# Attention heads of a hybrid encoder: a new order on VectorE and ScalarE, and second copies read from SBUF

## What is computed

```python
proj = h @ w_in                                # h is (528, 1024), w_in (1024, 3072)
q, k, v = split(proj, 3)                       # 8 heads; q, k: 2 components of 64; v: 128
for s0 in range(0, L, Q_BLOCK):
    mask = cid[None, :ke] <= cid[s0:e0, None]  # chunks of 64 tokens, block-causal
    sc = einsum('bqhcd,bkhcd->bhcqk', q[:, s0:e0], k[:, :ke])
    p = softmax(where(mask, sc, -inf), axis=-1)
    attn = p[:, :, 0] - lam * p[:, :, 1]
    outs.append(einsum('bhqk,bkhe->bqhe', attn, v[:, :ke]))
o = o * rsqrt(mean(o * o, axis=-1) + SUBLN_EPS)
o = o * head_gain * (1.0 - lambda_init)
return o @ w_out
```

## Time and profile before

| | |
|---|---|
| median of 3 runs | 1328.1 us (1328.01 to 1328.35) |
| the profiled execution, own time | 1331.93 us |
| its span | 1330.3 us |
| mean granted TensorE clock | 0.991 |
| TensorE busy | 1262.3 us, 95% |
| VectorE busy | 701.1 us, 53% |
| ScalarE busy | 562.1 us, 42% |
| GpSimd busy | 77.5 us, 6% |

### The profile page before, as it was taken

How to read it: one execution, slowest core, us unless ns; L and a number is a source line. 1 busy time by engine, 2 the same in 40 slices (tenths; PEclk the granted TensorE clock), 3 DMA queues, 4 the chain that set the end, 5 groups by cost and what they waited for, 6 DMA issues and landing times.

```text
span 1330.3 us, 20889 instructions
## 1 busy us (share of the span) xinstructions
PE 1262.3 (95%) x8341; PEld 1151.7 (87%) x8341; DVE 701.1 (53%) x1034; ACT 562.1 (42%) x927; POOL 77.5 (6%) x104
## 2 busy tenths in 40 slices
PE   7899999999999999999988888888999999999997
PEld 6899999999999999999977777776788888888886
DVE  5867777654334334345556666664744343343443
ACT  4556656534123123133355666664542232231333
POOL 3311221110000000000100000000000000000000
PEclk9899999999999999999999999999999999999999
DMA  6342251222323222222321111121323223232221
GB/s 163 91 102 75 64 117 65 84 80 96 96 69 100 87 95 95 95 67 91 95 64 49 48 47 47 47 63 49 95 93 97 86 99 101 86 103 95 81 77 64
DMA packets 141574, 110.28 MB, mean 83 GB/s; under 512 B 22104, under 2 KB 139920, under 8 KB 141520
## 3 DMA queue, kind: packets, MB, share of 16 engines
q1 hardware_dynamic: 140000, 104.93, 25.7%
q0 software_dynamic: 1392, 4.49, 1.5%
q10 hardware_dynamic: 128, 0.09, 0.0%
HBM read 107.38 MB, written 2.13 MB: 82 GB/s over the span
## 4 chain that ended last, share of the span: by engine, by line
PE 74%; issue 20%; DVE 3%; ACT 1%; POOL 0%; DMA 0%; DVEq 0%; POOLq 0%; ACTq 0%
PE ps L1282 70%; PE ps L1331 3%; PE ps L1348 1%; DVE wl L864 0%; DMA meta_in<-in_meta_tokens_dram 0%; DVE yl L906 0%; PE ps L1380 0%; PE ps L1412 0%; DVE plo L973 0%; PE ps L1401 0%; PE ps L1434 0%; PE ps L1298 0%; DVE h L891 0%; DVE dmat L962 0%; DVE fin L1264 0%
## 5 line engine op out<-in xcount | busy, mean ns | idle before, releaser
L1282 PE MATMUL ps<-yh,wh 128*128 128x264 f32 (+1 forms) x1472 | 368.9, 314 | 1.4 <-DVE wl L864 0.8
L1282 PE MATMUL ps<-yl,wh 128*128 128x264 f32 (+1 forms) x1472 | 362.6, 310 | 0.0
L1282 PE MATMUL ps<-yh,wl 128*128 128x264 f32 (+1 forms) x1472 | 361.7, 310 | 0.0
L504 ACT ACTIVATE wh<-raw 128x1024 fp32r<-128x1024 f32 x192 | 200.2, 1050 | 189.1 <-PE ps L1282 188.7
L864 DVE TENSOR_TENSOR wl<-raw,wh 128x1024 fp32r<-128x1024 f32 x192 | 240.4, 1256 | 58.2 <-ACT wh L504 56.1
L1282 PE MATMUL ps<-ah,wh 128*128 128x264 f32 (+1 forms) x960 | 258.0, 323 | 1.5 <-DVE al L1253 0.8
L1282 PE MATMUL ps<-al,wh 128*128 128x264 f32 (+1 forms) x960 | 257.4, 322 | 0.0
L1282 PE MATMUL ps<-ah,wl 128*128 128x264 f32 (+1 forms) x960 | 256.5, 321 | 0.0
L1282 PEld LDWEIGHTS ps<-yh,wh 128*128 128x128 f32 x1472 | 240.9, 190 | 17.9 <-issue 2.1
L1282 PEld LDWEIGHTS ps<-yl,wh 128*128 128x128 f32 x1472 | 240.6, 190 | 13.1 <-issue 0.2
L1282 PEld LDWEIGHTS ps<-yh,wl 128*128 128x128 f32 x1472 | 240.1, 190 | 13.6
(11 more groups left out here) (213 smaller groups left out, 1086.8 us busy)
## 6 DMA issues: line engine op xcount, KB each, us to landing
raw<-in_mlp_w_up_dram SPq DMA_DIRECT2D x32, 1024.0 KB, 5.3
raw<-in_mlp_w_down_dram SPq DMA_DIRECT2D x32, 1024.0 KB, 4.9
raw<-in_diff_w_in_dram SPq DMA_DIRECT2D x24, 512.0 KB, 3.7
raw<-in_mlstm_w_in_dram SPq DMA_DIRECT2D x16, 512.0 KB, 3.9
raw<-in_mlstm_w_in_dram SPq DMA_DIRECT2D x16, 256.0 KB, 4.2
raw<-in_mlstm_w_out_dram SPq DMA_DIRECT2D x3, 1024.0 KB, 4.8
raw<-in_diff_w_out_dram SPq DMA_DIRECT2D x3, 1024.0 KB, 4.9
mbc<-gate_rows POOLq DMA_DIRECT2D x8, 264.0 KB, 4.4
```

Of the source, the lines that this page charges most:

```text
L504: return nc.scalar.activation(o, i, ACT.Copy, scale=scale)
L1282: last = mm(ps[:, bank + s, 0:w_], w[:, slot, kb, :], m[:, kb, t0:t0 + w_], start=(kb == 0 and n == 0), stop=(kb == CB - 1 and n == 2))
```

## The change

The diff of the kernel. In words: ScalarE's second copies of `vmeta` and `att_meta` read the first copy in SBUF and wait for it, with semaphores of their own (`vm_dup`, `meta_dup`) that TensorE waits for, while `vt_rd1` and `meta_rd` are now raised by the first copies. On ScalarE `qm` and the next q's weight split move behind the exponentials of block 2, and `turned` of block 2 ahead of the second `keys_hi`. On VectorE the maxima of block 0 and the low half of block 3 move to the end of the step before; meta's low half goes before the v weights' split; q's evacuation goes between the maxima and the weights of block 1; the maxima of block 2 go before `qlo`; the split of the next q's weights goes behind the maxima of block 3. On TensorE one more block of q is done ahead of the scores of block 1, and the last one directly behind them, before `output`.

```diff
--- before.py
+++ after.py
@@ -287,8 +287,8 @@
         max_done = [sem(f"max_done{c}") for c in range(2)]
         exp_done = [sem(f"exp_done{c}") for c in range(2)]
         rden_rd, e1_rd, attn_rd, at_t, at_rd, atl_rd = sems("rden_rd e1_rd attn_rd at_t at_rd atl_rd")
-        mask_base, mask_half, mask_made, qm_done, vtl_rd1, metal_rd = sems(
-            "mask_base mask_half mask_made qm_done vtl_rd1 metal_rd")
+        mask_base, mask_half, mask_made, qm_done, vtl_rd1, metal_rd, vm_rd1, vm_dup, meta_dup = sems(
+            "mask_base mask_half mask_made qm_done vtl_rd1 metal_rd vm_rd1 vm_dup meta_dup")
         lam_dve, lam_act = sems("lam_dve lam_act")
 
         hg_done, fsum, fln, frs, fmul_act, fmul_dve = sems("hg_done fsum fln frs fmul_act fmul_dve")
@@ -767,9 +767,10 @@
                 if exists(hd):
 
                     act.wait_ge(v_t1, hd + 1)
-                    copy(vth1[par][:, :, :], ps[:, B_TR1, :].rearrange("p (s e) -> p s e", e=P))
-                    copy(vmeta[par][0:16, :], ps[0:16, B_TR1 + 1, 0:P])
-                    copy(vmeta[par][32:48, :], ps[0:16, B_TR1 + 1, 0:P]).then_inc(vt_rd1, 1)
+                    copy(vth1[par][:, :, :], ps[:, B_TR1, :].rearrange("p (s e) -> p s e", e=P)).then_inc(vt_rd1, 1)
+                    copy(vmeta[par][0:16, :], ps[0:16, B_TR1 + 1, 0:P]).then_inc(vm_rd1, 1)
+                    act.wait_ge(vm_rd1, hd + 1)
+                    copy(vmeta[par][32:48, :], vmeta[par][0:16, :].bitcast(F32)).then_inc(vm_dup, 1)
                     if exists(n1):
                         split_unit(n1 * 3 + (U_IN1 + 2), 2, 1, n1)
                     else:
@@ -779,8 +780,9 @@
                 if exists(hd - 1):
 
                     act.wait_ge(meta_t, hd)
-                    copy(att_meta[0:16, :], ps[0:NMETA, B_TR1, :])
-                    copy(att_meta[64:80, :], ps[0:NMETA, B_TR1, :]).then_inc(meta_rd, 1)
+                    copy(att_meta[0:16, :], ps[0:NMETA, B_TR1, :]).then_inc(meta_rd, 1)
+                    act.wait_ge(meta_rd, hd)
+                    copy(att_meta[64:80, :], att_meta[0:16, :].bitcast(F32)).then_inc(meta_dup, 1)
                 if exists(hd):
                     for c in range(2):
                         scores(hd * 4 + 1, 1, c)
@@ -803,6 +805,11 @@
                         b0 = 64 * c
                         last = copy(qst[1 - par][c][b0:b0 + 64, :], qf1[b0:b0 + 64, NMETA:T], SCORE_SCALE)
                     last.then_inc(qhi_done, 1)
+                if exists(hd):
+                    for c in range(2):
+                        scores(hd * 4 + 2, 2, c)
+                    turned(hd, hd * 4 + 1, 1)
+                if exists(n1):
                     for c in range(2):
                         b0 = 64 * c
                         last = copy(qm[1 - par][c][b0:b0 + 64, :], qf1[b0:b0 + 64, NMETA:T], SCORE_SCALE)
@@ -810,10 +817,6 @@
                     split_unit(n1 * 3 + (U_IN1 + 3), 0, 1, n1 + 1)
                 elif exists(hd):
                     split(U_OUT1 + 3, 3, 1)
-                if exists(hd):
-                    for c in range(2):
-                        scores(hd * 4 + 2, 2, c)
-                    turned(hd, hd * 4 + 1, 1)
                 if exists(n1):
 
                     act.wait_ge(evac, n1 * 3 + (U_IN1 + 2))
@@ -821,10 +824,9 @@
                 if exists(hd):
                     for c in range(2):
                         scores(hd * 4 + 3, 3, c)
+                    turned(hd, hd * 4 + 2, 2)
                 if exists(n1):
                     keys_hi(par, 1)
-                if exists(hd):
-                    turned(hd, hd * 4 + 2, 2)
                 if exists(hd - 1):
 
                     act.wait_ge(ssq_done1, hd)
@@ -1177,6 +1179,7 @@
                 dve.wait_ge(vt_rd1, hd + 1)
                 V.tensor_tensor(vtl1[par][:, :, :], ps[:, B_TR1, :].rearrange("p (s e) -> p s e", e=P),
                                 vth1[par][:, :, :].bitcast(F32), ALU.subtract)
+                dve.wait_ge(vm_rd1, hd + 1)
                 V.tensor_tensor(vmeta[par][64:80, :], ps[0:16, B_TR1 + 1, 0:P],
                                 vmeta[par][0:16, :].bitcast(F32), ALU.subtract).then_inc(vtl_rd1, 1)
 
@@ -1189,39 +1192,32 @@
             def step1(hd, par, pair):
                 n1 = hd + 1
                 if exists(hd):
-                    maxima(hd * 4, 0)
-                if exists(hd - 1):
-                    turned_lo(hd * 4 - 1, 3)
-                if exists(hd):
                     values_lo(hd, par)
                     weights(hd, hd * 4, 0)
+                if exists(hd - 1):
+                    meta_lo(hd - 1)
                 if exists(n1) and exists(hd):
                     split(n1 * 3 + (U_IN1 + 2), 2)
                 elif exists(hd):
                     split(U_OUT1 + 2, 2)
-                if exists(hd - 1):
-                    meta_lo(hd - 1)
                 if exists(hd):
                     maxima(hd * 4 + 1, 1)
-                    weights(hd, hd * 4 + 1, 1)
                 if exists(n1):
 
                     scaled(n1 * 3 + U_IN1, 0, SEQ, qf1[:, :],
                            ps[:, 4 if isinstance(hd, int) and hd < 0 else B_Q1, :])
                 if exists(hd):
+                    weights(hd, hd * 4 + 1, 1)
                     turned_lo(hd * 4, 0)
+                    maxima(hd * 4 + 2, 2)
                 if exists(n1):
-                    split(n1 * 3 + (U_IN1 + 3), 0)
                     dve.wait_ge(qhi_done, n1 + 1)
                     for c in range(2):
                         b0, b1 = 64 * c, 64 - 64 * c
                         last = V.scalar_tensor_tensor(qst[1 - par][c][b1:b1 + 64, :], qf1[b0:b0 + 64, NMETA:T], SCORE_SCALE,
                                                       qst[1 - par][c][b0:b0 + 64, :].bitcast(F32), ALU.mult, ALU.subtract)
                     last.then_inc(qlo_done, 1)
-                elif exists(hd):
-                    split(U_OUT1 + 3, 3)
-                if exists(hd):
-                    maxima(hd * 4 + 2, 2)
+                if exists(hd):
                     weights(hd, hd * 4 + 2, 2)
                     turned_lo(hd * 4 + 1, 1)
                 if exists(n1):
@@ -1231,6 +1227,9 @@
                     maxima(hd * 4 + 3, 3)
                 if exists(n1):
                     keys_lo(n1, par, 0)
+                    split(n1 * 3 + (U_IN1 + 3), 0)
+                elif exists(hd):
+                    split(U_OUT1 + 3, 3)
                 if exists(hd):
                     weights(hd, hd * 4 + 3, 3)
                 if exists(n1):
@@ -1246,6 +1245,10 @@
                     wait(dve, v_t1, n1)
                     scaled(n1 * 3 + (U_IN1 + 2), 0, ALL, vf1[:, :],
                            ps[:, 2:4, 0:HALF] if isinstance(hd, int) and hd < 0 else None)
+                    maxima(n1 * 4, 0)
+                if exists(hd):
+                    turned_lo(hd * 4 + 3, 3)
+                if exists(n1):
                     split(n1 * 3 + (U_IN1 + 4), 1)
                 if exists(hd - 1):
 
@@ -1509,6 +1512,8 @@
             def output(n, par):
 
                 pe.wait_ge(metal_rd, n + 1)
+                pe.wait_ge(meta_dup, n + 1)
+                pe.wait_ge(vm_dup, n + 1)
                 mm(ps[:, B_PV1, :], vmeta[par][:, :], att_meta[:, :], start=True, stop=False)
                 for s in range(4):
                     for m, (v, w) in enumerate(((vth1, ath), (vth1, atl), (vtl1, ath))):
@@ -1583,18 +1588,19 @@
                         out_part(3, 0, 3)
                 if exists(hd):
                     if nxt:
-                        part(n1, 0, 5, 6)
+                        part(n1, 0, 5, 7)
                     scores(hd * 4 + 1, 1, par)
-                if exists(hd - 1):
-                    output(hd - 1, 1 - par)
-                if exists(hd):
                     if nxt:
-                        part(n1, 0, 6, CB)
+                        part(n1, 0, 7, CB)
                     elif last_head:
                         out_part(0, 5, 6)
                         out_part(1, 0, 1)
+                if exists(hd - 1):
+                    output(hd - 1, 1 - par)
+                if exists(hd):
 
                     wait(pe, metal_rd, hd)
+                    wait(pe, meta_dup, hd)
                     wait(pe, vtl_rd1, hd + 1)
                     turn(hd * 4, 0)
                 if nxt:
```

More of the change, by code:

```diff
@@ L1585, in step1 @@
                     if nxt:
-                        part(n1, 0, 5, 6)
+                        part(n1, 0, 5, 7)
                     scores(hd * 4 + 1, 1, par)
+                    if nxt:
+                        part(n1, 0, 7, CB)
+                    elif last_head:
+                        out_part(0, 5, 6)
+                        out_part(1, 0, 1)
                 if exists(hd - 1):
@@ L1590, in step1 @@
                 if exists(hd):
-                    if nxt:
-                        part(n1, 0, 6, CB)
-                    elif last_head:
-                        out_part(0, 5, 6)
```

(2 more changed lines are left out.)

## The result

The changed kernel takes 1280.67 us in the median (1280.51 to 1282.83, 4 runs), the kernel before 1328.22 us: a ratio of 0.9641, 95% interval 0.9623 to 0.9658. The direction held, and the stalls went as forecast, though the one before the product not by the filler that was given for it. One term, the pure work of a head, was 1 us too large, and it counts seven times.

A forecast was written before the change was run, and what follows sets the result against it. TensorE was taken as the only engine near its limit, losing time to stalls in the attention heads. Gains of 0.75 + 6.3 + 4.0 + 24.1 + 4.7 = 39.9 us took 1328.1 to 1288.2 us, range 1282 to 1306.

The forecast's parts named there:

- the pure work of a head: Steady head on TensorE: length of 31.27 us less 5.2 us standing still, taken as 26.05 us.
- Maxima of block 0 and low half of block 3: Value turning starts 2.6 us after the head's first scores (L), against 4.05; its stall shrinks from 1.62 to 0.1-0.2 us.
- Copies: ScalarE's second value and meta copies, reading SBUF: 0 to 0.3 us more ScalarE time per head, 0.2 taken, beside other work.
- Filler: Six more matmuls before block 1's scores, three after: product 3.1 us after the meta turning (M), its 1.18 us stall gone.
- Block 1's turn: TensorE turning block 1's weights: a new stall of 0.5 us a head, bounds 0 and 1.0.
- Block 2: Earlier maxima and exponentials remove stalls of 1.46 us before block 3's scores and 0.77 before turning block 2's weights.
- The ends: Gains outside heads 2 to 6: 0.75 us before head 0, 6.3 in it, 4.0 in head 1, 4.7 in the last.
- 1 (the clock falls all the same): Clock still falls in head 0 or the last head, costing 2.7 or some 1.7 us: 1291 to 1293 us, chance 12%.
- 2 (stalls half return): Slipping queues bring back 2 to 2.5 us a head, 14 to 18 over seven heads: 1302 to 1306 us, chance 18%.
- 3 (no change): ScalarE and VectorE with their waits form their own loop of about 31 us a head: 1328 us, chance 3%.
- 4 (slower by block 1's turn): Wait before turning block 1's weights grows past about 2.5 us and the clock may fall: 1335 us, chance 5%.
- no new stall, 26.0 a head: Fast end of the forecast case (chance 62%): no new wait in a head, 26.0 us each, 1283 us in all.

The follow-up runs named there:

- k_block_earlier: Changed kernel with a third block of k ahead of block 2's scores instead of behind block 1's turn: 1277.27 us, ratio 0.9614 to the kernel before.
- undo_maxima0: Changed kernel with maxima of block 0 and block 3's low half put back to the start of VectorE's step: 1288.64 us.
- filler_and_q_undone: Changed kernel with TensorE's q blocks put back and q's evacuation back behind block 1's weights on VectorE: 1281.79 us.
- only_block2: Kernel before with block 2's new order on ScalarE and VectorE alone: 1300.45 us, ratio 0.9782.
- undo_filler: Changed kernel with TensorE's q blocks put back, one before block 1's scores and two behind the product: 1286.99 us.
- undo_block2: Changed kernel with block 2's old order put back on ScalarE and VectorE: 1315.0 us, ratio 0.9894 to the kernel before.
- only_maxima0: Kernel before with the maxima of block 0 and block 3's low half moved alone: 1320.05 us, ratio 0.9947.

## Why the prediction was wrong

**The step that failed** is "Pure work is thus 31.27 - 5.2 = 26.05 us", and with it each stretch taken over as its length before less its bracket. The pure work is 25.39 - 0.36 = 25.03 at most, and k_block_earlier runs a whole head in 24.81. Stretch by stretch the forecast was 2.5, 2.8, 8.1, 4.8, 1.8 and 6.45; measured are 2.48, 2.66, 7.99, 4.66, 1.43 and 6.17. The last two make over half of the error of 1.06, for a reason that the rows of the kernel before show when read for starts. TensorE, then VectorE:

```profile
759.87 0.39 PE L1532 MATMUL ps<-sqh,head_mean 128*128 128x512 f32 x1
...
761.88 0.48 PE L1282 MATMUL ps<-yh,wh 128*128 128x264 f32 x2
```

```profile
761.03 0.70 DVE L883 TENSOR_TENSOR kf<-ps,rb 128x528 f32<-128x528 f32 x1
```

Block 2's turn starts at 761.26 and the v part 0.62 us later; after, it is 0.25. The v part waits for k's evacuation, until 761.73, and no bracket tells of it, since the turns' rows reach over the gap. The scores of block 3 took 759.87 - 758.70 = 1.17 us, against 0.97 after (739.91 to 740.88). Half of the 0.20 lies behind the first matmul, half behind the first one of the second component (759.29 to 759.50, where 0.12 is usual), whose exponentials ended at 759.22: by these times it waited for them, again without a bracket. The rest, 0.15 to 0.2 a stall, is a pipeline that empties and fills: an L1285 matmul of 512 columns lasts 0.39 and the next starts 0.23 after it. That is a reading; k_block_earlier, with 0.22 us beside the bracket, is the one clean measurement of it.

Point by point:

- *Maxima of block 0 and low half of block 3*: right, 2.48 for L + 2.6, and limited by ScalarE's copy as said (it ends at 723.77, the low half behind it at 724.49, and the turning starts at 724.60). undo_maxima0 prices it at 8.2 us.
- *Copies*: taken at nothing, with bounds of 0 to 0.3 against the change. They gained 0.27 us a head and 3.0 in all. The early release was named, with 0.6 us; its effect on the values' low half was not counted. The source, SBUF for PSUM, won nothing by the rows above; a run with one of the two alone was not made. The pair of 1.19 us that the prediction takes for 128x512 copies is of 16x512 ones.
- *Filler*: the product's stall went, as said, but filler_and_q_undone shows that it goes without the filler too, but for 0.2 us. The earlier meta low half did it, by its place and by the first copy's release. The prediction had the numbers: its low half ends at M + 1.95, and without the moved filler the product could start at 2.98 - 1.18 = M + 1.8.
- *Block 1's turn*: a new stall of 0.5 was forecast, 0.36 came, released by atl.
- *Block 2*: right in place and cause. It is the largest part, 28.1 us alone and 33.1 when undone from the whole. Its two gains without a bracket, above, were not seen.
- *The ends*: before head 0, 0.9 for 0.75. Head 0 takes 21.40 us for 22.7; the 2.7 of the clock came back, with the same 1 us of pure work too much, and the 0.4 that was counted at block 1's turn did not come (no bracket there). Head 1 is 25.36. The last head is 26.62 to its product, for 27.2 to 28. It still holds 2.6 us of idle time; 1.50 of it stand before its own meta turning, which waits for the low half of block 3, as many as before.
- *Rivals.* 1 (the clock falls all the same): it did not, in head 0 or in the last. In only_block2, whose head 0 has no stall above 0.87 us inside it, it stayed up there too. The argument against this rival, that a fall comes only behind several stalls close together, was a wrong reading for head 0: before, the clock fell at 696.0, ahead of the second stall, which began at 697.34 - 1.10 = 696.24. 2 (stalls half return): not as built, but undo_filler is that case, with the q evacuation ahead of the weights as its cause; it costs 6 us, not 14 to 18. 3 (no change): it did not come. 4 (slower by block 1's turn): the stall stayed at 0.36.

The range was closed below at "no new stall, 26.0 a head", a bound made of the very number that was off. An error in the pure work could only add to the gain, and no case stood for it.

## What to carry to other kernels

Price a stall of a pipelined engine by the distance of starts, compared with the same run of instructions where nothing waits, not by the idle time in the row. Ahead of a filled engine, order each helper queue by which result the engine needs next, and put splits and copies that are needed late behind them; then check each move against the others, since one of them can cost time beside an old order: here q's evacuation ahead of the weights, with the old filler, costs 5 us (undo_filler against filler_and_q_undone). A stall that is left after such a change may be covered by shifting a block of filler, here for 3.4 us.

## What the runs showed of the hardware

A scaling on VectorE with its operands in SBUF took 1.31 us in place of 0.42 when GpSimd subtracted two SBUF tiles at the same time (undo_filler): it began at 761.91 and ended at 763.22, GpSimd's operation at 763.06. The Trainium skill, page "GPSIMD Engine Reference", section "Key points", says that the two engines share their SBUF interfaces, and that VectorE's instructions in a 2-port mode or with two SBUF inputs contend with GpSimd. These rows agree that they contend; in which mode the scaling ran, no row shows. Here the price is 0.89 of the 1.15 us in which the two ran together, and much the same in all six heads where they meet (1.28 to 1.31 us).

The granted clock fell from 2.4 to 1.2 GHz around the end of a stall of 1.9 to 2.6 us. Before, in head 0, the stall of 2.54 us ended at 694.96 and the clock fell at 696.0, with the stall of 1.10 still to come:

```profile
695.90:696.00 0.10, 0.10 (x3) 0.09 (x1) 0.10 (x1) 0.00 (x0) 0.00 (x0) 1.00 0.02 5
696.00:696.10 0.10, 0.10 (x2) 0.00 (x0) 0.10 (x1) 0.00 (x0) 0.00 (x0) 0.58 0.00 0
```

In heads 1, 2, 4 and 5 of undo_block2 it fell at 720.4, 751.2, 809.2 and 839.9, where stalls of 2.20 or 2.21 us ended at 718.80, 750.41, 809.47 and 838.87, each time before a second stall began. In the last head before, it fell at 904.2; a stall of 1.90 us had ended at 902.76, behind stalls of 0.44 and 0.74 in the same head. Only in head 0 of only_maxima0 did it fall within a second stall: at 693.9, with 2.56 us idle up to 692.16 and 1.14 up to 694.54. The page "TensorE: Matmul & The Clock Gate" of the Trainium skill, in "HAM oscillation — how this bites in real kernels", speaks of one long gap; the rows agree so far that such a gap, here of 1.9 to 2.6 us, went ahead of each fall, and that in head 0 before and in undo_block2 no second one was needed after it. But heads 3 and 6 of undo_block2, with gaps of 2.18 and 2.21 us, had no fall. What decides between the heads was not settled.
